# Two reorderings in a two-layer encoder kernel: the last chunk's activations before the last weight unit in every expert, and retention values projected feature-first, then turned

## The chip, the cores and the metric

The kernel runs on one core of one Trainium2 chip. The metric is the time of one execution in device microseconds, the median of several runs. Engines are called PE (TensorE's matmuls), PEld (TensorE's weight loads), DVE (VectorE), ACT (ScalarE), POOL (GpSimd) and SP (SyncE, which issues nearly all DMAs here).

## The reference

A trunk of two layers over 272 tokens (16 meta tokens and 256 frames) of width 1024. Each layer has a block with four retention heads and four latent-attention heads side by side, then a SwiGLU feed-forward; layer 0's is dense, layer 1's has 8 experts of which each token takes 2. Cut to what matters here:

```python
for layer in range(DEPTH):
    hn = rms_norm(h_res, attn_norm[layer])
    proj = hn @ w_in[layer]
    r_q, r_k, r_v, r_g, c_q, c_kv, k_rope = jnp.split(proj, IN_SPLITS, axis=-1)
    rv = to_heads(r_v, RET_HEADS)                     # the retention values
    y_ret = from_heads(head_rms(retention(rq, rk, rv)))
    y_mla = latent_attention(c_q, c_kv, k_rope, ...)  # softmax attention
    h_res = h_res + jnp.concatenate([y_ret * ..., y_mla * ...], axis=-1) @ w_out[layer]
    hn = rms_norm(h_res, ffn_norm[layer])
    # layer 0: dense; layer 1:
    for e in range(N_EXPERTS):
        out = out + gate_dense[..., e:e+1] * ((silu(hn @ w_gate[e]) * (hn @ w_up[e])) @ w_down[e])
```

## The kernel before, in words

**Numbers in two parts.** Every fp32 product is made of three fp32r matmuls (`mm3`): a high part times a high part, low times high, high times low. So each weight unit that comes from memory, 128 x 2048 numbers (1 MB), is first split: ACT copies it to `w_hi` (L919 in the attention and the dense part, L1110 in the experts), and DVE subtracts that copy from the unit and writes `w_lo` (L1178 and L1454). There are three split slots (`HSLOTS`). ACT may write a slot once PE has finished the unit that lay there (`w_used`), and PE may begin a unit once DVE has counted it in `split_lo`. SP refills a ring slot when the low part of its old unit is made. The engines run their own written order; nothing is scheduled by a tool.

**An expert** (8 of them, one after the other) takes its up to 128 tokens through 7 chunks of 512 hidden features. A chunk has four gate and up units (`g`, `u`) and two down units (`d`), of 12 matmuls of 512 columns each. PE's order is gate(c), transposes of the activations of chunk c-1 (`turn_hidden`), up(c), down(c-1); after chunk 6 only down(6) is left. The activations are made as gate x up by DVE (`a_moe`, L1466), turned by four PE transposes (`turn_hidden`, which signals `at_done`), copied to a high part by ACT (`hidden`, L1114) and given a low part by DVE (`hidden`, L1459, which signals `e_a`). down(c) waits for that. In the last chunk PE's order is: unit d(5,0); `turn_hidden(6)` and `turn_rows` (the next expert's tokens, 8 transposes); unit d(5,1); d(6,0); d(6,1). ACT and DVE go through one list of units, three ahead of PE: at the place of d(5,0) they split the last unit d(6,1) (`high_of`, `low_of`), then make the activations' parts (`hidden(6)`), then the next expert's tokens' parts (`take`, L1100 and L1438).

**The attention part of a layer.** Projections put features on partitions and 272 tokens in columns (`proj`: 24 matmuls of 272 columns, weights stationary), into a ring of four PSUM banks (`rot_bank`), from which ACT copies them out (`keep`, L957). The retention values are the exception: they are wanted with tokens on partitions, so `rv` is made in three token tiles (128, 128 and 16 tokens), each with the token tile stationary and 512 weight columns moving, 24 matmuls a tile. Between the tiles PE computes `latent_scores(2)` and `(3)`, on which DVE runs `mask_max` (L1240 to L1245) and ACT `exps` (L983); DVE's `normalise` (L1249, L1252) then makes them ready for `prob_transposes`, which follow the third tile on PE. After that come `proj("g0")`, the second transposes, and so on.

Of the kernel before, what the change touches and what calls it, by code (L numbers as in the profile page):

```python
# [41 lines left out]
P = 128  # L42
D = 1024
DK = D // P
# [5 lines left out]
HEADS = 4  # L50
# [10 lines left out]
UNIT = 2048  # L61
# [14 lines left out]
MOE_CHUNKS = DFF // 512  # L76
# [3 lines left out]
U_UQ, U_UKV, U_RV, U_RG, U_T1, U_T2, U_WO = 6, 7, 8, 10, 12, 13, 14  # L80
# [13 lines left out]
TILES = [(META, P), (META + P, P), (0, META)]  # L94
# [1 line left out]

OUTS = (["ckv", "kpe", "cq0", "cq1", "q0", "sckv", "scq", "q1", "q2", "q3", "k0", "k1", "k2", "k3",
# [3 lines left out]
N_OUTS = len(OUTS)  # L101

# [43 lines left out]
def build(nc, stream, h0, gains, router_w, fnorm, consts, out):  # L146
    with ExitStack() as ctx:
# [15 lines left out]
        hi = parts[:, 0:8 * L].rearrange("p (k t) -> p k t", k=8)  # L163
        lo = parts[:, 8 * L:16 * L].rearrange("p (k t) -> p k t", k=8)
# [28 lines left out]
        at = [0]  # L193
# [12 lines left out]
        rv, vm = carve3(3, 512), carve3(3, 512)  # L206
# [4 lines left out]
        std = carve3(HEADS, L)  # L211
# [37 lines left out]
        direct_used, split_hi, split_lo, w_used = sem("direct_used"), sem("split_hi"), sem("split_lo"), sem("w_used")  # L249
# [12 lines left out]
        out_done, out_free = sem("out_done"), sem("out_free")  # L262
# [49 lines left out]
        def split(eng, unit):  # L312

            n = SPLIT_OF[unit]
            eng.wait_ge(split_lo, n + 1)
            return w_hi[:, n % HSLOTS, :], w_lo[:, n % HSLOTS, :]
# [4 lines left out]
        def o_(name, layer):  # L321
            return layer * N_OUTS + OUTS.index(name)
# [150 lines left out]
        def _(pe):  # L473
            used_up = []
# [16 lines left out]
            def mm3(dst, sta, mov, start, stop, inc=None):  # L491

                mm(dst, sta[0], mov[0], start, False)
                mm(dst, sta[1], mov[0], False, False)
                mm(dst, sta[0], mov[1], False, stop, inc)
# [12 lines left out]
            def attention(layer):  # L508
                u0 = base_of(layer)
# [47 lines left out]
                def latent_scores(h):  # L557

                    dst = bank[6 + h % 2]
                    if h >= 2:  # L560
                        pe.wait_ge(sc_free, HEADS * layer + h - 1)
                    if h == 0:
                        pe.wait_ge(rope_done, N_ROPES * (layer + 1))
                        pe.wait_ge(out_free, o_("kn3", layer) + 1)
                    x = 64 * (h % 2)
                    for t, (c0, n) in enumerate([(0, META + P), (META + P, L), (MASK, META)]):
                        d = dst[0:TILES[t][1], c0:c0 + n]
                        mm(d, tok_rows(qn[:, h, :], t), kn[:, h, 0:n], True, False)
                        mm(d, tok_rows(qpe[x:x + 64, h // 2, :], t), kpe[x:x + 64, 0:n], False, True,
                           sc_done if t == 2 else None)  # L570
# [79 lines left out]
                w = slot(u0 + U_UKV)  # L650
                for h in range(HEADS):
                    mm(rot_bank(f"kn{h}"), w[:, h * P:(h + 1) * P], ckv, True, True, out_done)
                for t in range(3):
                    dst = rot_bank(f"v{t}", 512)[0:TILES[t][1], :]
                    mm(dst, tok_rows(ckv, t), w[:, 512:1024], True, True, out_done)
                used_up.append((direct_used, 1))
                latent_scores(0)
                latent_scores(1)
                for t in range(3):

                    p0 = TILES[t][0]
                    dst = rot_bank(f"rv{t}", 512)
                    for k in range(DK):
                        w = [x.rearrange("p (k c) -> p k c", k=4)[:, k % 4, :] for x in split(pe, u0 + U_RV + k // 4)]
                        mm3(dst, [hi[:, k, p0:p0 + P], lo[:, k, p0:p0 + P]], w, k == 0, k == DK - 1,
                            out_done if k == DK - 1 else None)
                    if t < 2:
                        latent_scores(2 + t)
                used_up.append((w_used, 2))
                prob_transposes(0)  # L670
                proj("g0", U_RG, 0)
                prob_transposes(1)
# [37 lines left out]
                p0 = 0 if layer == 0 else META  # L710
# [200 lines left out]
        def _(act):  # L911
# [36 lines left out]
            def attention(layer):  # L948
# [30 lines left out]
                def exps(h):  # L979
                    act.wait_ge(p1_ready, HEADS * layer + h + 1)  # L980
                    p = p_of(h)
                    for t, (rows, c0, c1) in enumerate([(P, 0, META + P), (P, META + P, MASK), (META, MASK, MASK + META)]):
                        x = A(p[0:rows, c0:c1], p[0:rows, c0:c1], ACT.Exp, bias=nmx[0:rows, h, t:t + 1], scale=SCALE,  # L983
                              accum_out=sums[0:rows, h, t:t + 1])
                    x.then_inc(exp_done, 1)
# [28 lines left out]
                    keep(f"v{t}", vm[0:rows, t, :], rows, 512)  # L1014
                exps(0)
                exps(1)
                for t, (_, rows) in enumerate(TILES):
                    keep(f"rv{t}", rv[0:rows, t, :], rows, 512)
                    if t < 2:
                        exps(2 + t)  # L1020
                high(b + 9)
                for name in OUTS[OUTS.index("g0"):]:
                    h = int(name[-1]) if name[-1].isdigit() else 0
# [78 lines left out]
            def expert(it):  # L1102
                def high_of(m):

                    n = MOE_SPLIT + m

                    act.wait_ge(slot_in[m % MOE_SLOTS], it * (16 * FFN_UNITS // MOE_SLOTS) + moe_arrivals(m))

                    act.wait_ge(w_used, it * FFN_UNITS + (n - HSLOTS + 1))
                    A(w_hi[:, n % HSLOTS, :], moe_slot(m), ACT.Copy).then_inc(split_hi, 1)  # L1110

                def hidden(c):
                    act.wait_ge(at_done, it * MOE_CHUNKS + c + 1)
                    A(ae_hi[c % 2], bank[6 if c < MOE_CHUNKS - 1 else 3][:, :], ACT.Copy).then_inc(e_ahi, 1)  # L1114

                scatter_copy(it)
                high_of(AHEAD)
                for m, (kind, c, i) in enumerate(MOE_ORDER[:-1]):
                    if (kind, i) == ("u", 1):
                        act.wait_ge(e_gu, it * MOE_CHUNKS + c + 1)  # L1120
                        A(sil_moe, bank[c % 2][:, :], ACT.Silu).then_inc(e_silu, 1)  # L1121
                    high_of(m + HSLOTS)
                    if (kind, i) == ("g", 1) and c:
                        hidden(c - 1)
                    if (kind, c, i) == ("d", MOE_CHUNKS - 2, 0):
                        hidden(c + 1)
                        take(it + 1)

            norm(0, mid=(0,), after=range(1, HSLOTS))
# [31 lines left out]
        def _(dve):  # L1161
# [43 lines left out]
            def attention(layer):  # L1205
                u0 = base_of(layer)
# [84 lines left out]
                    rope(r)  # L1291
                dve.wait_ge(ones_set, 4)
                arrived(dve, u0 + U_T1)
                for h in range(HEADS):
                    mask_max(h)
                for h in range(HEADS):
                    normalise(h)
                low(b + 9)
                low(b + 10)
# [8 lines left out]
                for h in range(HEADS):  # L1308
                    m = qn[:, h, :]
                    dve.wait_ge(out_free, o_(f"bM{h}", layer) + 1)  # L1310
                    x = V.scalar_tensor_tensor(out=m, in0=m, scalar=gain(G_MLA + 4 * layer + h), in1=std[:, h, :],
                                               op0=ALU.mult, op1=ALU.mult)
# [6 lines left out]
                for h in range(HEADS):  # L1319
                    m = qT[:, h, :]  # L1320
                    x = V.scalar_tensor_tensor(out=m, in0=m, scalar=gain(G_RET + 4 * layer + h), in1=rg[:, h, :],
                                               op0=ALU.mult, op1=ALU.mult)
# [8 lines left out]
                p0 = 0 if layer == 0 else META  # L1331
# [116 lines left out]
            def expert(it):  # L1448

                def low_of(m):  # L1450

                    n = MOE_SPLIT + m
                    dve.wait_ge(split_hi, it * FFN_UNITS + (n + 1))
                    V.tensor_tensor(w_lo[:, n % HSLOTS, :], moe_slot(m), w_hi[:, n % HSLOTS, :].bitcast(F32),  # L1454
                                    ALU.subtract).then_inc(split_lo, 1)

                def hidden(c):
                    dve.wait_ge(e_ahi, it * MOE_CHUNKS + c + 1)
                    V.tensor_tensor(ae_lo[c % 2], bank[6 if c < MOE_CHUNKS - 1 else 3][:, :], ae_hi[c % 2].bitcast(F32),  # L1459
                                    ALU.subtract).then_inc(e_a, 1)  # L1460

                low_of(AHEAD)
                for m, (kind, c, i) in enumerate(MOE_ORDER[:-1]):
                    if (kind, i) == ("u", 1):
                        dve.wait_ge(e_silu, it * MOE_CHUNKS + c + 1)
                        V.tensor_tensor(a_moe, bank[2 + c % 2][:, :], sil_moe, ALU.mult).then_inc(e_af, 1)  # L1466
                    low_of(m + HSLOTS)
                    if (kind, i) == ("g", 1) and c:
                        hidden(c - 1)
                    if (kind, c, i) == ("d", MOE_CHUNKS - 2, 0):  # L1470
                        hidden(c + 1)
                        take(it + 1)

            link(V.memset(rot, 0.0))
# [16 lines left out]
            for t in range(2):  # L1491
                x = V.tensor_scalar(G[:, t, :], col(C_IOTA, CAP), nxt[:, t:t + 1], None, ALU.is_equal)  # L1492
# [122 lines left out]
```

## Time and profile before

| | |
|---|---|
| median of 3 runs | 1569.68 us (1568.22 to 1570.18) |
| the profiled execution | 1569.67 us |
| its span, first to last instruction | 1567.9 us |
| PE busy | 1533.8 us, 98% of the span |
| DVE busy / ACT busy | 1207.4 us / 1010.3 us |
| mean granted TensorE clock | 0.996 of full |
| attention, layer 0 and layer 1 | about 15 to 162 us and 465 to 576 us |
| experts | 588 to 1551 us, one every 120.4 us |

How to read it: times in rows are microseconds from the start of the span. "Busy" of PE counts from the start of a matmul to its modelled end, and neighbours overlap: a matmul of 512 columns lasts 0.39 us in the records while the next one starts 0.23 us after it. So the distance from one start to the next is what a matmul costs in a row of them, and an idle time is read from starts.

### The profile page before, as it was taken

How to read it: one execution, taken by the hardware profiler on the slowest of the kernel's cores; microseconds unless marked ns; L12 is line 12 of the kernel's file. 1: busy time of each engine (PE TensorE's matmuls, PEld its weight loads, DVE VectorE, ACT ScalarE, POOL GpSimd, SP SyncE). 2: the span in 40 equal slices, each digit the busy share in tenths (PEclk: the TensorE clock that was granted, in tenths of full speed). 3: DMA queues.
4: the chain of work that ended last, by engine and by line, in shares of the span. 5: the costliest groups of instructions: out<-in, count | busy, mean ns of one | idle time of the engine just before them, and what ended most of it. 6: DMA issues, size and time to landing. Idle time of an engine off the chain costs nothing.

```text
span 1567.9 us, 21768 instructions
## 1 busy us (share of the span) xinstructions
PE 1533.8 (98%) x8368; PEld 1314.9 (84%) x8368; DVE 1207.4 (77%) x1015; ACT 1010.3 (64%) x938; POOL 35.3 (2%) x41
## 2 busy tenths in 40 slices
PE   9999999999999999999999999999999999999997
PEld 8778899999996798888887887887887887887885
DVE  5735566656684468888898888888888988888887
ACT  5645443333464557777777777777777777777775
POOL 0000000000000003000000000000000000000000
PEclk9999999999999999999999999999999999999998
DMA  8314444454333249999999999999999999999992
GB/s 335 133 69 162 149 175 161 164 191 184 128 122 134 90 155 363 397 350 391 370 355 388 372 361 385 381 355 377 372 376 365 384 376 354 394 376 348 420 359 109
DMA packets 64563, 447.91 MB, mean 286 GB/s; under 512 B 8105, under 2 KB 8137, under 8 KB 12160
## 3 DMA queue, kind: packets, MB, share of 16 engines
q1 hardware_dynamic: 61200, 438.02, 72.3%
q0 software_dynamic: 3312, 9.18, 2.1%
q8 instruction: 36, 0.59, 0.1%
q14 instruction: 15, 0.12, 0.0%
HBM read 442.20 MB, written 7.36 MB: 287 GB/s over the span
## 4 chain that ended last, share of the span: by engine, by line
PE 90%; DVE 4%; ACT 4%; issue 2%; DVEq 0%; ACTq 0%; POOL 0%; POOLq 0%
PE bank L485 88%; ACT w_hi L1110 2%; PE bank L489 2%; DVE w_lo L1454 1%; DVE sq L1195 0%; DVE scratch L1184 0%; DVE parts L1459 0%; ACT w_hi L919 0%; ACT scratch L1094 0%; DVE w_lo L1178 0%; DVE parts L1190 0%; ACT scratch L975 0%; ACT scratch L976 0%; DVE scratch L1403 0%; ACT scratch L957 0%
## 5 line engine op out<-in xcount | busy, mean ns | idle before, releaser
L485 PE MATMUL bank<-w_hi,parts 128*128 128x512 f32 x2784 | 866.3, 392 | 12.0 <-DVE parts L1459 8.8
L1454 DVE TENSOR_TENSOR w_lo<-ring,w_hi 128x2048 fp32r<-128x2048 f32 x288 | 659.7, 2293 | 105.2 <-ACT w_hi L1110 101.8
L1110 ACT ACTIVATE w_hi<-ring 128x2048 fp32r<-128x2048 f32 x288 | 551.9, 1919 | 187.3 <-PE bank L485 159.9
L485 PEld LDWEIGHTS bank<-w_hi,parts 128*128 128x128 f32 x2784 | 516.8, 188 | 123.2 <-DVE w_lo L1454 16.9
L485 PE MATMUL bank<-w_lo,parts 128*128 128x512 f32 x1392 | 542.9, 390 | 0.0
L485 PE MATMUL bank<-parts,w_hi 128*128 128x272 f32 (+1 forms) x2112 | 405.7, 290 | 6.1 <-DVE parts L1190 2.5
L485 PEld LDWEIGHTS bank<-parts,w_hi 128*128 128x128 f32 x2112 | 332.1, 188 | 9.0 <-DVE parts L1190 3.1
L485 PEld LDWEIGHTS bank<-w_lo,parts 128*128 128x128 f32 x1392 | 261.3, 188 | 55.5
L485 PE MATMUL bank<-parts,w_lo 128*128 128x272 f32 (+1 forms) x1056 | 303.3, 287 | 0.0
L1178 DVE TENSOR_TENSOR w_lo<-ring,w_hi 128x2048 fp32r<-128x2048 f32 x72 | 163.5, 2288 | 73.2 <-ACT w_hi L919 73.2
L485 PEld LDWEIGHTS bank<-parts,w_lo 128*128 128x128 f32 x1056 | 199.0, 188 | 0.4
L919 ACT ACTIVATE w_hi<-ring 128x2048 fp32r<-128x2048 f32 x72 | 137.5, 1912 | 89.8 <-PE bank L485 89.6
L1454 DVE TENSOR_TENSOR w_lo<-hT,w_hi 128x2048 fp32r<-128x2048 f32 x48 | 110.2, 2295 | 11.1 <-ACT w_hi L1110 9.2
L1110 ACT ACTIVATE w_hi<-hT 128x2048 fp32r<-128x2048 f32 x48 | 92.1, 1918 | 22.5 <-PE bank L485 13.6
L485 PE MATMUL bank<-scratch 128*128 128x128 f32 (+10 forms) x280 | 63.6, 355 | 1.3 <-issue 0.8
L485 PEld LDWEIGHTS bank<-scratch 128*128 128x128 f32 (+4 forms) x280 | 38.9, 175 | 28.4 <-issue 16.4
L1344 DVE TENSOR_TENSOR hT<-hT,bank 128x272 f32<-128x272 f32 x112 | 47.4, 435 | 16.8 <-PE bank L485 15.0
L1121 ACT ACTIVATE scratch<-bank 128x512 f32<-128x512 f32 x56 | 33.6, 599 | 32.1 <-PE bank L485 32.1
L489 PEld LDWEIGHTS bank<-c_sb,scratch 128*128 128x128 f32 x290 | 35.0, 141 | 10.5 <-issue 3.3
L489 PE MATMUL bank<-c_sb,scratch 128*128 128x128 f32 x290 | 40.9, 272 | 2.9 <-DVE scratch L1492 2.9
L1059 ACT ACTIVATE scratch<-bank 128x272 f32<-128x272 f32 x14 | 5.6, 398 | 54.0 <-PE bank L485 54.0
L1466 DVE TENSOR_TENSOR scratch<-bank,scratch 128x512 f32<-128x512 f32 x56 | 38.3, 685 | 0.0
(160 smaller groups left out, 626.6 us busy)
## 6 DMA issues: line engine op xcount, KB each, us to landing
ring<-stream SPq DMA_DIRECT2D x360, 1024.0 KB, 6.6
hT<-stream SPq DMA_DIRECT2D x48, 1024.0 KB, 7.0
ring<-stream SPq DMA_DIRECT2D x2, 976.0 KB, 4.7
ring<-stream SPq DMA_DIRECT2D x2, 768.0 KB, 9.9
c_sb<-consts SPq DMA_DIRECT2D x1, 1136.0 KB, 10.5
hT<-h SPq DMA_DIRECT2D x2, 544.0 KB, 4.4
ring<-stream SPq DMA_DIRECT2D x2, 544.0 KB
ring<-stream SPq DMA_DIRECT2D x2, 512.0 KB
```

What stands on the lines that cost most here:

```text
L485: return release(nc.tensor.matmul(dst, lhsT, rhs, start=start, stop=stop), inc)
L489: return release(nc.tensor.transpose(dst, src, ident[0:n, 0:n]), inc)
L919: A(w_hi[:, n % HSLOTS, :], slot(UNIT_OF[n]), ACT.Copy).then_inc(split_hi, 1)
L1059: A(sil_dense[:, 0, :], bank[0][:, 0:L], ACT.Silu)
L1110: A(w_hi[:, n % HSLOTS, :], moe_slot(m), ACT.Copy).then_inc(split_hi, 1)
L1121: A(sil_moe, bank[c % 2][:, :], ACT.Silu).then_inc(e_silu, 1)
L1178: V.tensor_tensor(w_lo[:, n % HSLOTS, :], slot(UNIT_OF[n]), w_hi[:, n % HSLOTS, :].bitcast(F32), ALU.subtract).then_inc(split_lo, 1)
L1344: V.tensor_tensor(hT[:, d, :], hT[:, d, :], bank[4 + d % 4][:, 0:L], ALU.add).then_inc(h_added, 1)
L1454: V.tensor_tensor(w_lo[:, n % HSLOTS, :], moe_slot(m), w_hi[:, n % HSLOTS, :].bitcast(F32), ALU.subtract).then_inc(split_lo, 1)
L1466: V.tensor_tensor(a_moe, bank[2 + c % 2][:, :], sil_moe, ALU.mult).then_inc(e_af, 1)
```

## The change

Three edits.

1. **Experts, last chunk.** At the place of unit d(5,0), ACT and DVE now first make the activations' parts (`hidden(6)`) and then split the last unit d(6,1); `take` stays third. PE's and SP's orders are the same.
2. **Retention values.** They are now projected like the others, head by head, weights stationary and 272 tokens moving (`rT0` to `rT3`, kept in `std`), and then turned by 12 PE transposes, four to each of the three token tiles. `latent_scores(2)` now comes after `rT1` and `latent_scores(3)` after `rT2`, and ACT's `exps(2)` and `exps(3)` behind the copies of `rT1` and `rT2`. The weights in memory are laid out to match. The two weight units are given back one by one (after `rT1` and `rT3`) instead of together.
3. **Softmax.** DVE's `normalise(0)` moves ahead of `mask_max(3)`.

```diff
+                for h in range(HEADS):
+                    proj(f"rT{h}", U_RV + h // 2, h % 2)
+                    if h in (1, 2):
+                        latent_scores(1 + h)
                 for t in range(3):
-                    p0 = TILES[t][0]
+                    p0, rows = TILES[t]
                     dst = rot_bank(f"rv{t}", 512)
-                    for k in range(DK):
-                        w = [... for x in split(pe, u0 + U_RV + k // 4)]
-                        mm3(dst, [hi[:, k, p0:p0 + P], lo[:, k, p0:p0 + P]], w, ...)
-                    if t < 2:
-                        latent_scores(2 + t)
-                used_up.append((w_used, 2))
+                    pe.wait_ge(out_free, o_("rT3", layer) + 1)
+                    for h in range(HEADS):
+                        turn(dst[0:rows, h * P:(h + 1) * P], std[:, h, p0:p0 + rows], ...)
...
+                for h in range(HEADS):
+                    keep(f"rT{h}", std[:, h, :])
+                    if h in (1, 2):
+                        exps(1 + h)
                 for t, (_, rows) in enumerate(TILES):
                     keep(f"rv{t}", rv[0:rows, t, :], rows, 512)
-                    if t < 2:
-                        exps(2 + t)
...  (ACT; the same edit with low_of on DVE)
+                    last = (kind, c, i) == ("d", MOE_CHUNKS - 2, 0)
+                    if last:
+                        hidden(c + 1)
                     high_of(m + HSLOTS)
                     if (kind, i) == ("g", 1) and c:
                         hidden(c - 1)
-                    if (kind, c, i) == ("d", MOE_CHUNKS - 2, 0):
-                        hidden(c + 1)
+                    if last:
                         take(it + 1)
...
-                for h in range(HEADS):
+                for h in range(HEADS - 1):
                     mask_max(h)
-                for h in range(HEADS):
+                normalise(0)
+                mask_max(HEADS - 1)
+                for h in range(1, HEADS):
                     normalise(h)
```

What stands in a row on ACT at the end of an expert before the change (bank3 holds the last chunk's turned activations, the `hT` ring slot the last unit, bank7 and bank6 the next expert's tokens):

```order
L1110 ACTIVATE w_hi<-ring 128x2048 [waits w_used]
L1107 REGISTER_ALU
L1109 REGISTER_ALU [waits slot_in6]
L1110 ACTIVATE w_hi<-hT 128x2048 [waits w_used]
L1114 ACTIVATE parts<-bank3 128x512 [waits at_done]
L1099 ISA
L1100 ACTIVATE parts<-bank7 128x512 [waits gt_done]
```

And after it:

```order
L1112 ACTIVATE w_hi<-ring 128x2048 [waits w_used]
L1116 ACTIVATE parts<-bank3 128x512 [waits at_done]
L1109 REGISTER_ALU
L1111 REGISTER_ALU [waits slot_in6]
L1112 ACTIVATE w_hi<-hT 128x2048 [waits w_used]
L1101 ISA
L1102 ACTIVATE parts<-bank7 128x512 [waits gt_done]
```

The copy of the activations has moved ahead of the last unit's copy; DVE's two subtractions have changed places in the same way, and each still stands behind ACT's copy of the same thing.

On PE, the end of the retention values before the change, the third token tile's last matmuls and the transposes behind it:

```order
L485 MATMUL bank<-w_hi,parts 128x512 x2
L485 MATMUL bank<-w_lo,parts 128x512
L489 MATMUL bank<-c_sb,sq 128x128 x3
L489 MATMUL bank<-c_sb,sq 16x16
L489 MATMUL bank<-c_sb,sq 16x128 x2
```

And after it, the last matmuls of `rT3`, the 12 new transposes (they read `std`, a part of `scratch`), and the old transposes of `sq`:

```order
L485 MATMUL bank<-parts,w_hi 128x272
L489 MATMUL bank<-c_sb,scratch 128x128 [waits out_free]
L489 MATMUL bank<-c_sb,scratch 128x128 x3
L489 MATMUL bank<-c_sb,scratch 128x128 [waits out_free]
L489 MATMUL bank<-c_sb,scratch 128x128 x3
L489 MATMUL bank<-c_sb,scratch 16x128 [waits out_free]
L489 MATMUL bank<-c_sb,scratch 16x128 x3
L489 MATMUL bank<-c_sb,sq 128x128 [waits p2_ready]
```

The new transposes stand between the last projection and the old ones, and the first of them waits for ACT's copy of `rT3`.

## Rows read from the trace of the kernel before

**Rows 1.** The page's busy times, with the share of the span and instructions.

```profile
PE 1533.8 (98%) x8368; PEld 1314.9 (84%) x8368; DVE 1207.4 (77%) x1015; ACT 1010.3 (64%) x938; POOL 35.3 (2%) x41
```

**Rows 2.** Waits of PE: engine, line <- waited for: us in total, times, longest.

```profile
PE bank L485 <- DVE parts L1459: 8.8, 8, 1.1
```

**Rows 3.** Timeline of PE, second expert's end: start, length, line, count.

```profile
818.64 1.47 PE L489 MATMUL bank<-c_sb,scratch 128*128 128x128 f32 x12
819.87 0.71 PE L485 MATMUL bank<-w_hi,parts 128*128 128x512 f32 x2
...
822.02 0.62 PE L485 MATMUL bank<-w_hi,parts 128*128 128x512 f32 x2
...
823.96 0.70 PE L485 MATMUL bank<-w_hi,parts 128*128 128x512 f32 x2 [1.10 <-DVE parts L1459]
...
824.73 0.62 PE L485 MATMUL bank<-w_hi,parts 128*128 128x512 f32 x2
...
829.50 0.62 PE L485 MATMUL bank<-w_hi,parts 128*128 128x512 f32 x2
```

**Rows 4.** Timeline of ACT, the same stretch.

```profile
818.95 1.93 ACT L1110 ACTIVATE w_hi<-hT 128x2048 fp32r<-128x2048 f32 x1 [0.43 <-PE bank L489]
820.77 0.58 ACT L1114 ACTIVATE parts<-bank 128x512 fp32r<-128x512 f32 x1
821.24 1.08 ACT L1100 ACTIVATE parts<-bank 128x512 fp32r<-128x512 f32 x2
824.47 1.92 ACT L1110 ACTIVATE w_hi<-ring 128x2048 fp32r<-128x2048 f32 x1 [2.14 <-PE bank L485]
```

**Rows 5.** Timeline of DVE, the same stretch.

```profile
818.55 2.29 DVE L1454 TENSOR_TENSOR w_lo<-ring,w_hi 128x2048 fp32r<-128x2048 f32 x1
820.90 2.31 DVE L1454 TENSOR_TENSOR w_lo<-hT,w_hi 128x2048 fp32r<-128x2048 f32 x1
823.13 0.68 DVE L1459 TENSOR_TENSOR parts<-bank,parts 128x512 fp32r<-128x512 f32 x1
823.74 1.27 DVE L1438 TENSOR_TENSOR parts<-bank,parts 128x512 fp32r<-128x512 f32 x2
826.42 2.29 DVE L1454 TENSOR_TENSOR w_lo<-ring,w_hi 128x2048 fp32r<-128x2048 f32 x1 [1.41 <-ACT w_hi L1110]
```

**Rows 6.** Timeline of PE in layer 0: retention values, transposes, projection g0.

```profile
73.25 0.73 PE L485 MATMUL bank<-w_hi,parts 128*128 128x512 f32 x2
...
89.32 0.73 PE L485 MATMUL bank<-w_hi,parts 128*128 128x512 f32 x2
...
94.99 0.92 PE L489 MATMUL bank<-c_sb,sq 128*128 128x128 f32 x6
95.66 0.37 PE L485 MATMUL bank<-parts,w_hi 128*128 128x272 f32 x1
...
98.76 0.92 PE L489 MATMUL bank<-c_sb,sq 128*128 128x128 f32 x6
```

**Rows 7.** Timeline of DVE and ACT in the same stretch: mask, exponentials, g0's copy.

```profile
89.42 0.59 DVE L1240 TENSOR_TENSOR sq<-bank,ring 128x416 f32<-128x416 f32 x1 [6.04 <-PE bank L485]
...
91.45 0.42 ACT L983 ACTIVATE sq<-sq,nmx 128x144 f32<-128x144 f32 x1 [3.71 <-DVE nmx L1245]
...
92.57 0.18 ACT L983 ACTIVATION_READ_ACCUMULATOR sq<-sq,nmx 16x1 f32 x1
...
98.96 0.40 ACT L957 ACTIVATE scratch<-bank 128x272 f32<-128x272 f32 x1 [1.39 <-PE bank L485]
```

**Rows 8.** Windows: stretch, length, busy of PE, PEld, DVE, ACT, POOL; PEclk, DMA share, GB/s.

```profile
579.00:582.00 3.00, 3.00 (x20) 3.00 (x20) 2.08 (x9) 2.55 (x4) 1.03 (x1) 0.67 0.08 11
714.98:835.32 120.34, 119.02 (x540) 98.07 (x540) 105.84 (x59) 89.44 (x60) 2.61 (x2) 1.00 0.98 371
840.00:850.00 10.00, 10.00 (x47) 8.27 (x46) 8.95 (x6) 7.29 (x6) 0.00 (x0) 1.00 1.01 417
```

More of the change, by code:

```diff
@@ L658, in attention @@
                 latent_scores(1)
+                for h in range(HEADS):
+                    proj(f"rT{h}", U_RV + h // 2, h % 2)
+                    if h in (1, 2):
+                        latent_scores(1 + h)
                 for t in range(3):
-                    p0 = TILES[t][0]
+                    p0, rows = TILES[t]
                     dst = rot_bank(f"rv{t}", 512)
-                    for k in range(DK):
-                        w = [x.rearrange("p (k c) -> p k c", k=4)[:, k % 4, :] for x in split(pe, u0 + U_RV + k // 4)]
-                        mm3(dst, [hi[:, k, p0:p0 + P], lo[:, k, p0:p0 + P]], w, k == 0, k == DK - 1,
-                            out_done if k == DK - 1 else None)
-                    if t < 2:
-                        latent_scores(2 + t)
-                used_up.append((w_used, 2))
+                    pe.wait_ge(out_free, o_("rT3", layer) + 1)
+                    for h in range(HEADS):
+                        turn(dst[0:rows, h * P:(h + 1) * P], std[:, h, p0:p0 + rows], out_done if h == HEADS - 1 else None)
                 prob_transposes(0)
@@ L1466, in expert @@
                         V.tensor_tensor(a_moe, bank[2 + c % 2][:, :], sil_moe, ALU.mult).then_inc(e_af, 1)
+                    last = (kind, c, i) == ("d", MOE_CHUNKS - 2, 0)
+                    if last:
+                        hidden(c + 1)
                     low_of(m + HSLOTS)
@@ L1469, in expert @@
                         hidden(c - 1)
-                    if (kind, c, i) == ("d", MOE_CHUNKS - 2, 0):
-                        hidden(c + 1)
+                    if last:
                         take(it + 1)
@@ L1570 @@
             units[at + 4 + i] = cols(rk[:, 256 * i:256 * (i + 1)])
-            units[at + U_RV + i] = rv[512 * i:512 * (i + 1)].reshape(4, P, 512).transpose(1, 0, 2).reshape(P, UNIT)
+            units[at + U_RV + i] = cols(rv[:, 256 * i:256 * (i + 1)])
             units[at + U_RG + i] = cols(rg[:, 256 * i:256 * (i + 1)])
```

2 rows, old and new, of the table OUTS are left out of this document.

## The prediction

> **What bounds the kernel now.** I began with the page's busy times: PE is busy for 98% of the span, DVE for 77%, ACT for 64% [rows 1]. Work that ACT or DVE saves is therefore worth nothing by itself. Time can be won in two ways only: fewer or shorter matmuls, or a pause of PE that goes away. The second view is the list of what PE waits for. One item stands above the rest: DVE's L1459, 8 waits of up to 1.1 us [rows 2], so one for each expert, at the same place. L1459 is the low part of the activations. The third view is the timeline of the three engines around one such wait [rows 3 to 5], and the fourth the stretch of layer 0 in which the retention values are made [rows 6, 7]. Last I looked at what the transfers and the clock do [rows 8].
>
> **Part 1: the experts' last chunk.** First the pause. The last triple of unit d(5,1) starts at 822.02 and the first of d(6,0) at 823.96. How fast triples follow in a row is seen between 824.73 and 829.50: 7 triples, 0.681 us each. Without a pause the second triple of d(6,0) would have started two triples behind 822.02, at 823.38; it started at 824.73 [rows 3]. The pause costs 1.35 us, somewhat more than the listed 1.1, because the matmul's modelled end hides a part and the first triple behind a pause is slower (0.77 us).
>
> What ends it? DVE finishes the last unit's low part at 823.21, then the activations' low part at 823.81 [rows 5], and PE starts 0.15 us later. The low part of d(6,0) itself was ready at 820.84 [rows 5]. So PE waits for the activations, and these stand on both engines behind the split of a unit that PE wants only a unit later.
>
> Now the new order, step by step. The 12 transposes take 818.64 to 819.87, 0.10 us each [rows 3]. ACT's split of the last unit starts at 818.95, on the first transpose's end [rows 4]; the fourth, which signals `at_done`, ends 0.31 us later, at 819.26. ACT copies the activations until 819.84 (0.58), then the last unit from 819.75 to 821.68 (1.93; neighbours on ACT overlap by 0.1), then the next tokens to 822.7 (1.08) [rows 4]. DVE is with d(6,0) until 820.84, makes the activations' low part until 821.5 (0.68), then the last unit's from 821.7 to 824.0 (2.31), then the tokens' until 825.2 (1.27) [rows 5]. PE reaches d(6,0) at 822.70 and finds everything ready for 1.2 us. It reaches d(6,1) 4 triples later, at 825.43, and the low part is there since 824.0. The pause is gone.
>
> What is late next? The next expert's first unit: ACT can start it 0.51 us behind the first matmul of d(6,0) (824.47 against 823.96 [rows 3, 4]), now at 823.21, so it is done at 825.1; DVE comes free at 825.2 and ends at 827.5; PE wants it at 829.50 - 1.35 = 828.15. A margin of 0.65 us, against 0.79 before (828.71 for 829.50 [rows 3, 5]). The units behind it hang on PE's own progress and keep their distance, and so does the wait that PE has at the third unit of the next expert. What queues behind the new wait for `at_done` on ACT is only the last unit's copy, on DVE only its subtraction, and these have 1.4 us to spare; SP refills that unit's slot 0.8 us later than now, with a whole round of seven slots before it is wanted. So 8 x 1.35 = **10.8 us**. From below the term is bounded by what the list of waits counts, 8.8 us; from above by nothing more than the pause.
>
> **Can the transfers follow?** An expert would take 119.0 us instead of 120.34, in which 371 GB/s are moved, with the DMA engines busy for 0.98 of it; at the same volume that asks for 375. In 840 to 850 the same queue moved 417 GB/s [rows 8]. I take the transfers for able to follow. The Trainium skill (DMA: Bandwidth & Descriptors, "Where 436 GB/s comes from") says that for transfers from HBM the memory side binds, near 358 GB/s for a core; by that rule the experts could not speed up at all. The trace disagrees by those two rows, but the rule is a rival below.
>
> **Part 2: the retention values.** A block of 24 matmuls of 512 columns takes from 89.32 to 94.99, 5.67 us, and there are three, the first from 73.25 [rows 6]; the third runs at full length although it has only 16 tokens. Removed: 17.0. Added: four blocks of 24 matmuls of 272 columns. Block g0 takes from 95.66 to 98.76, 3.10 us [rows 6]: 12.4. The two score computations between the blocks are as before. The 12 transposes have their like at the experts' end, 1.23 us [rows 3].
>
> Between `rT3` and the first transpose PE waits for ACT's copy. For g0 that copy starts 0.20 us behind the block's end and lasts 0.40 [rows 6, 7]. But `exps(3)` stand ahead of it: the scores end at 89.32, the mask begins at 89.42, the exponentials run from 91.45 to 92.75 [rows 7], 3.43 us behind the scores. The block takes 3.10, so the copy starts 0.33 behind the block instead of 0.20, ends at 0.73, and PE goes on at about **0.75**. `normalise(0)`, now ahead of that mask on DVE, falls into the 6.04 us for which DVE idles there [rows 7]; it costs nothing, and it brings nothing, since the transposes that want it come 3 us later. Where that cover fails it costs the 0.8 us it lasts.
>
> Behind the transposes, ACT copies three tiles out and splits a unit, some 3.7 us, and `g0`'s copy is wanted over 5 us behind the first transpose; the four new copies of `rT` fall where ACT has nothing to do. Each layer: 17.0 - 12.4 - 1.23 - 0.75 = 2.6 us. PE is what ends this stretch and nearly all after it, so I count it in full, twice: **5.2 us**. Bounds: 0 if what follows holds the same end, 6.7 with no pause at all.
>
> **The sum.** 10.8 + 5.2 = 16.0 from the profiled execution's 1569.67 gives 1553.7; the median of the runs, 1569.68, is the same.
>
> **The rivals.**
> A. *The attention's gain is lost*: once PE comes earlier, something that does not move with it is late, such as a transfer of tables or of the output weights. For it: there is nothing I can show. Against: the units that follow were loaded long before. 1569.67 - 10.8 = 1558.9.
> B. *The next expert's first unit takes the pause's place.* Its margin is the smallest I found, 0.65 us, and rests on DVE's chain of last unit, tokens, first unit. If it is late by 0.5 us the experts give 8 x 0.85 = 6.8 and the sum is 1557.7.
> C. *The transfers bind* and an expert stays at 120.34 us: only 5.2 are won, 1564.5. For it: 0.98 busy. Against: 417 GB/s.
> D. *The clock falls* at the pause before the transposes. In 579 to 582, behind a wait and a few tiny matmuls, the granted clock was 0.67, a mixture of 2.4 and 1.2 GHz [rows 8]. Two thirds of 3 us at the lower level and the like of it behind cost under 2 us each time, twice a kernel: 1557.5. Against: the new pause is shorter and stands among dense blocks. The Trainium skill (TensorE: Matmul & The Clock Gate, "What's actually happening") calls the lower clock the state of rest that activity lifts; the row agrees.
> E. *Slower*: the last unit, now second, and what is chained to it on DVE come later than I have them. Place: the end of each expert. Price: 8 us for each us beyond the margin of 0.65. It eats the whole gain at 2.0 us beyond, and passes +0.2% at 2.4; with 2.5 the time is 1573.7. Against: the row durations would have to be wrong by 3 us in a chain of 6.
>
> That the change doesn't do what it says would need PE to wait for the unit d(6,0) and not for the activations; its low part was 3.1 us old when PE started, so I leave that at next to nothing, inside C.
>
> **How the numbers follow.** Chances: the forecast 0.72 (1551.5 to 1556), A 0.08, B 0.08, C 0.04, D 0.04, E 0.04. The forecast's case with A, B and D makes 0.92; the range of 1551.5 to 1560 holds them, and I take 0.8 of it for sure since in each case the size may be off. A measurement of this kernel tells some 0.2%, 3.1 us, from no change. All cases but E lie beyond that on the fast side, C by 5 us; I leave 0.02 for no difference, 0.04 for slower, 0.94 for faster.
>
> **What would show it.** Part 1: PE's waits for the activations' low part are gone from its list, PE's triples run on from d(5,1) to d(6,0), and an expert takes 119.0 us. If B holds, PE waits 8 times at an expert's first unit. If C holds, ACT waits for DMAs. Part 2: from the first matmul of `rT0` to the transposes of the probabilities 19.1 us instead of 21.7; a wait of 0.75 us for the copy before the new transposes; the same in layer 1. The prediction is wrong if 512-column blocks are gone and the layer is no shorter.

## The result and the profile after

The changed kernel takes 1554.09 us (median of 4 executions, 1553.72 to 1556.38), the kernel before, on the same chip and in turn with it, 1569.93 (4 executions, 1568.22 to 1571.46). The ratio is 0.9902, with an interval of 0.9885 to 0.9920: 15.4 us less, between 12.6 and 18.1. The prediction's 16.0 lies in that. The profiled execution of after is the one of 1553.72 us; its span is 1551.9.

The page's busy times, answering to [rows 1]:

```profile
PE 1525.3 (98%) x8440; PEld 1314.6 (85%) x8440; DVE 1206.1 (78%) x1015; ACT 1012.5 (65%) x946; POOL 35.0 (2%) x41
```

PE has 72 matmuls more and is busy for 8.5 us less, and its share of the span is still 98%. So of the 16.0 us between the two profiled executions about half is shorter work and the other half is time in which PE stood still. The page alone does not say more.

The list of what PE waits for (in all, times, longest) answers to [rows 2]:

```profile
PE bank L489 <- DVE scratch L1500: 2.9, 1, 2.9
...
PE bank L485 <- DVE w_lo L1460: 1.5, 7, 0.2
PE bank L489 <- ACT scratch L957: 1.2, 2, 0.6
```

The item that led it, the activations' low part (L1465 now), is not in it at all. New is the last line: two waits of 0.6 us, one in each layer, for the copy ahead of the new transposes. The 7 waits of 0.2 us, at an expert's third unit, were there before.

**The experts.** PE's timeline at the second expert's end, answering to [rows 3] (start, length, line, count, idle before):

```profile
811.19 1.47 PE L489 MATMUL bank<-c_sb,scratch 128*128 128x128 f32 x12
812.42 0.70 PE L485 MATMUL bank<-w_hi,parts 128*128 128x512 f32 x2
...
815.25 0.61 PE L485 MATMUL bank<-w_hi,parts 128*128 128x512 f32 x2
...
820.69 0.61 PE L485 MATMUL bank<-w_hi,parts 128*128 128x512 f32 x2
...
825.45 0.61 PE L485 MATMUL bank<-w_hi,parts 128*128 128x512 f32 x2
...
826.50 0.73 PE L485 MATMUL bank<-w_hi,parts 128*128 128x512 f32 x2 [0.22 <-DVE w_lo L1460]
```

From the first triple of d(5,1), at 812.42, to 825.45 the triples follow each other every 0.68 us (the first takes 0.77), and no row between them has a wait; d(6,0) begins at 815.25. The next pause is the 0.22 us at 826.50, the third unit of the next expert. ACT and DVE in the same stretch, answering to [rows 4, 5]:

```profile
811.83 0.60 ACT L1116 ACTIVATE parts<-bank 128x512 fp32r<-128x512 f32 x1 [0.76 <-PE bank L489]
812.32 1.91 ACT L1112 ACTIVATE w_hi<-hT 128x2048 fp32r<-128x2048 f32 x1
...
815.67 1.92 ACT L1112 ACTIVATE w_hi<-ring 128x2048 fp32r<-128x2048 f32 x1 [0.47 <-PE bank L485]
```

```profile
813.31 0.69 DVE L1465 TENSOR_TENSOR parts<-bank,parts 128x512 fp32r<-128x512 f32 x1
814.26 2.29 DVE L1460 TENSOR_TENSOR w_lo<-hT,w_hi 128x2048 fp32r<-128x2048 f32 x1 [0.26 <-ACT w_hi L1112]
...
817.67 2.28 DVE L1460 TENSOR_TENSOR w_lo<-ring,w_hi 128x2048 fp32r<-128x2048 f32 x1
```

The activations' low part ends at 814.00, and PE wants it at 815.25. The next expert's first unit ends at 819.95 and PE wants it at 820.69: a margin of 0.7 us. What an expert takes is the distance between equal pieces of the chain of work. Of before, then of after (start, length, what):

```profile
714.98 11.20 PE bank L485 x48
...
1437.15 11.20 PE bank L485 x48
```

```profile
707.54 11.20 PE bank L485 x48
...
1421.40 11.20 PE bank L485 x48
```

Over the six experts between the first and the last of these, before took 120.36 each and after 118.98: 1.38 us less. Over the eight that is 11.1 us.

**The retention values.** PE's timeline of layer 0, answering to [rows 6], and ACT's, to [rows 7]:

```profile
89.26 0.29 PE L485 MATMUL bank<-parts,w_hi 128*128 128x272 f32 x1
90.13 1.50 PE L489 MATMUL bank<-c_sb,scratch 128*128 128x128 f32 x12 [0.58 <-ACT scratch L957]
91.47 0.92 PE L489 MATMUL bank<-c_sb,sq 128*128 128x128 f32 x6
```

```profile
89.51 0.19 ACT L983 ACTIVATION_READ_ACCUMULATOR sq<-sq,nmx 16x1 f32 x1
89.60 0.38 ACT L957 ACTIVATE scratch<-bank 128x272 f32<-128x272 f32 x1
```

The last matmul of `rT3` starts at 89.26, 0.13 us before the next could, and the transposes start at 90.13: a pause of 0.74. It ends with ACT's copy of `rT3`. In ACT's order that copy stands behind the six instructions of `exps(3)`, but it came hardly later for them: it starts 0.21 us behind the block's end (89.39), and g0's copy of before, ahead of which ACT was idle, started 0.20 us behind its block's end [rows 6, 7]. The pause is thus 0.21 us to the copy's start, 0.38 for the copy, and 0.15 from its end to the first transpose. From the first matmul of `rT0`, at 72.23, to the transposes of the probabilities, at 91.47, it is 19.24 us, where the prediction had 19.1 and before took 21.74. The whole stretch, in the chain of work of before and of after:

```profile
64.50 30.65 PE bank L485 x130
...
95.91 3.02 PE bank L485 x24
```

```profile
63.49 22.85 PE bank L485 x130
...
90.13 2.26 PE bank L489 x18
92.38 3.02 PE bank L485 x24
```

From the same first matmul to the end of g0's block: 34.43 us before, 31.91 after, so 2.52 less. In layer 1 the same pieces give 34.44 (478.96 to 513.40) and 31.92 (475.45 to 507.37).

**The account.** 11.1 + 2 x 2.52 = 16.1 of the 15.95 us between the two profiled executions. The rest are two stretches that the change does not touch, and that nearly cancel. At the start, the first piece of the chain is shorter, by 0.96 us; at the end, the last matmuls are longer, by 0.83, and so are the two transposes ahead of them, by 0.25 (0.66 instead of 0.41). 16.1 + 0.96 - 0.83 - 0.25 = 16.0, the difference of the spans. The first two rows are of before, the others of after:

```profile
1.13 8.80 PE bank L485 x36
...
1555.68 5.41 PE bank L485 x8
```

```profile
1.13 7.84 PE bank L485 x36
...
1538.84 6.24 PE bank L485 x8
```

The end is the clock: in the 8 us around those last matmuls the mean granted clock was 0.79 of full before and 0.57 after, mixtures of 2.4 and 1.2 GHz in both. For the start the clock's rows show nothing, 1.00 in both; it stays unexplained. A kernel with the attention of before (`e3_vector_swap_only`, below) also had the shorter start.

**The transfers.** One expert of after, answering to the second of [rows 8] (stretch, length, busy of PE, PEld, DVE, ACT, POOL; clock, DMA share, GB/s):

```profile
707.54:826.50 118.96, 118.75 (x540) 98.13 (x540) 105.69 (x59) 89.45 (x60) 2.62 (x2) 1.00 0.96 377
```

377 GB/s where 371 were moved before, and no wait for a DMA appeared. The Trainium skill (DMA: Bandwidth & Descriptors, "Where 436 GB/s comes from") has the memory side bind near 358 GB/s for a core; the measurement, on a chip of which one core runs, disagrees.

### The profile page after: what moved, and what is told of

The parts are those of the page before. It is cut to its first block, busy times and chain, and to the rows that moved or that the text cites. A ratio compares the mean times of both kernels' runs of the same rounds, so it can differ in the third digit from the quotient of the medians.

```text
span 1551.9 us, 21926 instructions
## 1 busy us (share of the span) xinstructions
PE 1525.3 (98%) x8440; PEld 1314.6 (85%) x8440; DVE 1206.1 (78%) x1015; ACT 1012.5 (65%) x946; POOL 35.0 (2%) x41
## 4 chain that ended last, share of the span: by engine, by line
PE 92%; DVE 4%; ACT 3%; issue 1%; ACTq 0%; DVEq 0%; POOL 0%; POOLq 0%
PE bank L485 89%; PE bank L489 3%; DVE w_lo L1460 1%; ACT w_hi L1112 1%; DVE sq L1199 0%; DVE scratch L1188 0%; ACT scratch L1096 0%; ACT w_hi L919 0%; DVE w_lo L1182 0%; DVE parts L1194 0%; ACT scratch L975 0%; ACT scratch L976 0%; DVE scratch L1409 0%; ACT scratch L957 0%; ACT sq L983 0%
## 5 line engine op out<-in xcount | busy, mean ns | idle before, releaser
L485 PE MATMUL bank<-w_hi,parts 128*128 128x512 f32 x2688 | 834.5, 392 | 3.3 <-DVE parts L1444 1.6
L485 PEld LDWEIGHTS bank<-w_hi,parts 128*128 128x128 f32 x2688 | 499.7, 188 | 108.0 <-DVE w_lo L1460 5.0
L485 PE MATMUL bank<-w_lo,parts 128*128 128x512 f32 x1344 | 523.8, 390 | 0.0
L485 PE MATMUL bank<-parts,w_hi 128*128 128x272 f32 (+1 forms) x2240 | 431.5, 291 | 6.1 <-DVE parts L1194 2.4
L485 PEld LDWEIGHTS bank<-parts,w_hi 128*128 128x128 f32 x2240 | 352.4, 188 | 9.2 <-DVE parts L1194 3.0
L485 PE MATMUL bank<-parts,w_lo 128*128 128x272 f32 (+1 forms) x1120 | 321.7, 287 | 0.0
L485 PEld LDWEIGHTS bank<-w_lo,parts 128*128 128x128 f32 x1344 | 252.2, 188 | 53.2
L485 PEld LDWEIGHTS bank<-parts,w_lo 128*128 128x128 f32 x1120 | 211.0, 188 | 0.4
L1112 ACT ACTIVATE w_hi<-hT 128x2048 fp32r<-128x2048 f32 x48 | 91.9, 1915 | 19.1 <-PE bank L485 13.7
L489 PE MATMUL bank<-c_sb,scratch 128*128 128x128 f32 (+1 forms) x314 | 44.1, 273 | 4.1 <-DVE scratch L1500 2.9
L489 PEld LDWEIGHTS bank<-c_sb,scratch 128*128 128x128 f32 (+1 forms) x314 | 37.4, 140 | 12.2 <-issue 3.3
```

The lines of the kernel that those rows point to most:

```text
L485: return release(nc.tensor.matmul(dst, lhsT, rhs, start=start, stop=stop), inc)
L489: return release(nc.tensor.transpose(dst, src, ident[0:n, 0:n]), inc)
```

## The experiments

All are timed in turn with the kernel before. Savings are (1 - ratio) x 1569.9. The first four take the change apart.

### The two parts alone

`e1_experts_only` is the kernel before with edit 1 alone (the new order on ACT and DVE); of this kernel only times are used. `e2_retention_only` is the kernel after with edit 1 undone on both engines:

```diff
-                    last = (kind, c, i) == ("d", MOE_CHUNKS - 2, 0)
-                    if last:
-                        hidden(c + 1)
                     high_of(m + HSLOTS)          # low_of on DVE
                     ...
-                    if last:
+                    if (kind, c, i) == ("d", MOE_CHUNKS - 2, 0):
+                        hidden(c + 1)
                         take(it + 1)
```

> The kernel before with the experts' edit alone (activations before the last unit, on ScalarE and VectorE). Theory, the two terms are separate and add: an expert takes 118.98 us instead of 120.37, 8 x 1.38 = 11.1 us less, so about 1558.8 against 1569.9. Rival, part of the experts' gain needed the attention's shift (another phase of the transfers): fewer than 8 us. Rival, the retention edit does all beyond 8.8 us: 1561.

> The kernel before with the retention values' and the softmax edit alone. Theory: 2.5 us less in each layer, 5.0 in all, 1564.9, and 8 waits of 1.1 us for the activations' low part still there. Rival, the layers' gain was luck of the clock at the start (the profile after began 1.0 us earlier before any edited line): then 1566 to 1570.

Measured: `e1_experts_only` 0.9931 [0.9919, 0.9943], 10.8 us less; `e2_retention_only` 0.9969 [0.9959, 0.9979], 4.9 us less. Predicted were 10.8 and 5.2. The two add up to 15.7, against 15.4 for both together, so neither part needs or spoils the other. In `e2_retention_only` PE's list of waits shows the old item, untouched:

```profile
PE bank L485 <- DVE parts L1463: 8.7, 8, 1.1
```

### One engine's order alone

Which engine's order made the pause? `e3_vector_swap_only` has the new order on DVE only, `e4_scalar_swap_only` on ACT only, both on the kernel before. The edit is the one of edit 1, in DVE's or in ACT's function.

> The kernel before with the experts' edit on VectorE alone; ScalarE still copies the last unit first. Theory, what holds TensorE is VectorE's 2.3 us subtraction of the last unit ahead of the activations': ScalarE's copy of the activations ends at 821.35 in the times of before, VectorE's subtraction at 822.05, TensorE wants it at 822.70. So the pause is gone with this half alone: as e1, 1558.8. Rival, both copies have to be swapped (the activations' copy on ScalarE is what comes late): a pause stays, 1563 to 1570.

> The kernel before with the experts' edit on ScalarE alone; VectorE still subtracts the last unit first, and now starts it 0.8 us later. Theory: the activations' low part ends at 824.7 instead of 823.8, the pause grows from 1.35 to 2.2 us: 8 x 0.87 = 7 us slower than before, 1576.9. Rival, the order on ScalarE is what counts: faster than before, down to 1559.

`e3_vector_swap_only`: 0.9936 [0.9923, 0.9949], 10.0 us less, not to be told from both orders together by the time. By its trace an expert takes 118.98 us (714.11 to 1428.00 for six), as in after. Its DVE timeline:

```profile
820.52 0.69 DVE L1459 TENSOR_TENSOR parts<-bank,parts 128x512 fp32r<-128x512 f32 x1 [0.53 <-ACT parts L1114]
```

ACT still makes the activations' copy 1.5 us later than in after (2.13 us behind the transposes' first start instead of 0.64), and DVE waits 0.53 us for it. But the low part ends at 821.21, and PE wants it at 821.84, where d(6,0) begins: 0.6 us to spare. So DVE's order alone is the cause of the pause and its cure; ACT's turns a spare 0.6 us into 1.2.

`e4_scalar_swap_only` went the other way: 1.0109 [1.0094, 1.0124], 17 us slower, where 7 had been expected. Its PE list of waits, PE's timeline at the second expert's end, and 12 us around that end (columns as above):

```profile
PE bank L485 <- DVE parts L1461: 15.1, 8, 1.9
```

```profile
826.12 0.70 PE L485 MATMUL bank<-w_hi,parts 128*128 128x512 f32 x2 [1.89 <-DVE parts L1461]
...
827.77 1.05 PE L485 MATMUL bank<-w_hi,parts 128*128 128x512 f32 x2
...
829.05 1.05 PE L485 MATMUL bank<-w_hi,parts 128*128 128x512 f32 x2
```

```profile
821.00:833.00 12.00, 10.12 (x40) 7.92 (x39) 7.68 (x7) 6.85 (x6) 1.03 (x1) 0.86 0.94 376
```

The expected part is there: the pause is listed with 1.9 us instead of 1.1, 8 times, and the experts without anything else take 121.14 us, 0.78 more than before (0.87 expected). The rest is the clock. From the third triple behind the pause they start 1.28 us apart (827.77, 829.05) instead of 0.68, which is the 1.2 GHz level, and the stretch had a mean granted clock of 0.86. It happened behind 3 of the 8 pauses; those experts took 122.77, so it cost 1.6 us each time. 8 x 0.78 + 3 x 1.6 = 11.0, and this profiled execution took 1581.4, 11.7 more than before's. The other executions took 1586 to 1589 at mean clocks of 0.988 to 0.991, against 0.992 here: more such falls, by the clock; they have no trace that shows where.

### The retention part's terms

`e5_normalise_back` undoes edit 3 alone, in after:

```diff
-                for h in range(HEADS - 1):
+                for h in range(HEADS):
                     mask_max(h)
-                normalise(0)
-                mask_max(HEADS - 1)
-                for h in range(1, HEADS):
+                for h in range(HEADS):
                     normalise(h)
```

> The changed kernel with the softmax order put back (all masks, then all normalisations). Theory, the move is free and idle: 1554.1, and the transposes of the probabilities wait for nothing, since the first normalisation would be done 1.2 us before they come. Rival, it carries part of the gain: up to 1.6 us more.

Measured: 0.9904 [0.9889, 0.9919], 1555.29 us. No change, as expected, and in its trace the stretch of layer 0 takes 31.91 us, as in after: edit 3 is worth nothing either way.

`e6_turns_twice` does the new transposes of every token tile twice (the second time the same results to the same place), which prices them by themselves:

```diff
-                    for h in range(HEADS):
-                        turn(dst[0:rows, ...], std[:, h, p0:p0 + rows], out_done if h == HEADS - 1 else None)
+                    for rep in range(2):
+                        for h in range(HEADS):
+                            turn(dst[0:rows, ...], std[:, h, p0:p0 + rows],
+                                 out_done if rep and h == HEADS - 1 else None)
```

> The changed kernel with the 12 new transposes of each layer done twice. Theory, they stand on the path at 1.34 us a dozen less what a pipeline start costs: 2 x 1.23 = 2.5 us more, 1556.6. Rival, they are partly hidden behind a later wait (for ScalarE's tables): 0 to 1 us more.

Measured: 0.9919 [0.9905, 0.9933], 1558.67 us, 2.7 less saved than after. The chain of work in layer 0:

```profile
90.91 3.57 PE bank L489 x30
```

30 transposes in 3.57 us against 18 in 2.26: 12 more cost 1.31 a layer, 0.109 each, in both layers 2.6. They lie in full on the path, as the sum had them, and are 0.1 us dearer than the 1.23 that was taken from the experts' end.

`e8_probs_before_turns` asks whether the pause before the transposes can be had for nothing, by putting the next matmuls of PE into it:

```diff
+                prob_transposes(0)
                 for t in range(3):
                     ...
-                prob_transposes(0)
```

> The changed kernel with the first transposes of the probabilities between the last projection and the new transposes. Theory: they fill 0.67 us of the 0.74 us for which TensorE waits for the copy: 2 x 0.65 = 1.3 us less, 1552.8. Rival, the new transposes then come 0.6 us later to ScalarE, and something behind is late: no gain.

In the trace the pause is gone. The chain of layer 0 runs through it: the 130 matmuls of after and the 24 of `rT3` are one piece.

```profile
64.27 26.06 PE bank L485 x154
...
92.41 3.03 PE bank L485 x24
```

From the same first matmul to the end of g0's block: 31.17 us, 0.74 less than after. Timed: 0.9894 [0.9881, 0.9908], by the ratios 1.3 us more saved than after, as 2 x 0.74 would have it; but the intervals overlap, and its median, 1554.84 us, is not below after's 1554.09, so the time proves no gain. The profiled execution shows where the 1.5 us went. In the matmuls ahead of the experts the granted clock was low (0.72 in 564 to 570), where after's was at full. The same 24 matmuls, of after and of this kernel:

```profile
566.73 2.84 PE bank L485 x24
```

```profile
566.00 4.35 PE bank L485 x24
```

### What is late next in an expert

The prediction gave the next expert's first unit a margin of 0.65 us and priced everything beyond at 8 us for each us (rivals B and E). Three kernels that are otherwise the kernel after put 1, 3 and 4 unused subtractions of 128 x 512 on DVE behind the tokens' parts, in `take` (0.6 us each):

```diff
+                for i in range(1):               # 3 and 4 in the others
+                    V.tensor_tensor(sq[:, 512 * i:512 * (i + 1)], bank[6][:, :], <x_hi, 512 columns>, ALU.subtract)
```

> The changed kernel with one more subtraction of 0.64 us on VectorE behind the next tokens' low part, ahead of the next expert's first unit (its result is used by nothing). That unit's low part ended 0.73 us before TensorE wanted it in the profile after. Theory, the margin is real: the experts take 118.98 us as before, and only the first, once, starts 0.6 us later: 1554.7. Rival, the experts' end is tighter than it looks: up to 5 us more.

> The same with three more, 1.83 us. Theory: the first unit comes 1.1 us late in each expert, 8 x 1.2 = 9.6 us more and 1.8 once: 1565.5. The pause is as long as the one of the kernel before, which left the clock alone, so the clock stays. Rival, the clock falls here too: 13 us more, 1578.

> The same with four more, 2.44 us: TensorE pauses 1.7 us at each expert's first unit. If the fall of the clock seen with ScalarE's half alone (a pause of 1.9 us, then triples of 1.28 us instead of 0.68) comes with the length of the pause: 8 x 1.8 + 2.4 + 8 x 1.6 = 30 us more, 1584. If that place or its transposes made it fall, not the length: 17 us more, 1571.

With one: 0.9899 [0.9882, 0.9915], 1554.4 us, and an expert takes 118.97 us. No change, so a margin of at least 0.6 is real. With three: 0.9952 [0.9936, 0.9969], 1563.2 us; with four: 0.9992 [0.9983, 1.0002], 1568.7 us. Both cost less than expected (1565.5, and 1571 at the least). PE's waits and the timeline, first with three, then with four:

```profile
PE bank L485 <- DVE w_lo L1463: 6.6, 7, 1.0
PE bank L485 <- DVE sq L1447: 4.2, 1, 4.2
PE bank L489 <- DVE scratch L1503: 4.2, 1, 4.2
```

```profile
825.05 0.62 PE L485 MATMUL bank<-w_hi,parts 128*128 128x512 f32 x2
...
826.84 0.73 PE L485 MATMUL bank<-w_hi,parts 128*128 128x512 f32 x2 [0.95 <-DVE w_lo L1463]
```

```profile
825.33 0.62 PE L485 MATMUL bank<-w_hi,parts 128*128 128x512 f32 x2
...
827.71 0.73 PE L485 MATMUL bank<-w_hi,parts 128*128 128x512 f32 x2 [1.54 <-DVE w_lo L1463]
```

The place is the one that rival B named, an expert's first unit. With three the unit starts 1.79 us behind the last triple instead of 0.68, so 1.11 late; with four 2.38, so 1.70 late. But an expert grew only by 0.72 (to 119.70) and by 1.32 (to 120.30, from 827.71 to 948.02). The difference is nearly the same in both, 0.39 and 0.38, and it is the wait that after has at the third unit: there the next triple starts 1.05 us behind 825.45 instead of 0.68, 0.37 late. That unit hangs on the end of the expert before, and where the first unit is late it comes in time: with three, one piece of the chain runs on for 72 matmuls through the place where after's chain begins anew.

```profile
826.84 16.62 PE bank L485 x72
```

So the first 0.37 us of lateness replace a wait that PE has anyway. The account with three, against after: the wait ahead of the first expert +2.6 (4.2 instead of 1.6), a lower clock behind it +2.0, seven experts 7 x 0.72 = +5.0; at the end a wait of 4.2 instead of 2.9, +1.3, the wait at the last expert's third unit -0.4, and shorter last matmuls (5.28 instead of 6.24, and the two before them) -1.2. Together 9.3, with 9.4 between the spans.

Nor did the clock fall inside the experts, with a listed pause of 1.5 us at seven places.

### Two better versions

`e7_unit_before_scatter` takes the wait at the third unit away. On ACT the unit is split ahead of the weighting of the last expert's output rows:

```diff
-                scatter_copy(it)
                 high_of(AHEAD)
+                scatter_copy(it)
```

> The changed kernel, and at each expert's start ScalarE copies the third unit before it scales the last expert's rows out. It aims at the wait left in each expert, between the third triple from the end of the second unit (825.45) and the next (826.50), 0.37 us, and the slow triple behind it, 0.13. Theory: the unit is ready 1.4 us earlier, the wait is gone, 8 x 0.5 = 4.0 us less, 1550.1. Rival, the rows' scaling, now late, delays what follows on ScalarE (the fourth unit): no gain or a loss of some us.

Measured: 1551.09 us, 0.9873 [0.9858, 0.9889], 19.9 saved, 4.6 more than after by the ratios and 3.0 less time by the medians. The chain runs through a whole expert without leaving PE; here is the piece over the place of the third unit's wait:

```profile
1051.62 24.54 PE bank L485 x108
```

An expert takes 118.46 us (1042.12 to 1160.58), 0.52 less than in after. There are seven such places, from the second expert on, so the trace carries 3.6 us; at the first expert's third unit a wait of 0.2 stays. `e11_both` has this edit and the one of `e8_probs_before_turns`:

> The changed kernel with both additions, the third unit before the rows' scaling and the first transposes of the probabilities before the new ones. Theory, they add: 4.3 us (an expert takes 118.46 instead of 118.98) and 1.5 us (0.75 in each layer), 0.9865 of before, 1548.5.

Measured: 1550.02 us (1549.36 to 1550.47), 0.9869 [0.9853, 0.9886], 20.6 saved. It has the lowest median, 4.1 us below after's, and none of its executions overlaps with after's; that it beats `e7_unit_before_scatter` is not shown, the intervals overlap nearly in full. Its expert takes 118.44 and its stretch in layer 0 is as in `e8_probs_before_turns`; a part was lost between, where its granted clock in the 25 us ahead of the experts was 0.86, like that of `e7_unit_before_scatter`, and after's 0.93.

## Why the prediction was right

- **What bounds the kernel.** PE, and only pauses or matmuls count. `e3_vector_swap_only` shows it best: ACT's order can be left as it was, DVE then waits 0.53 us, and nothing is lost.
- **The pause and what ends it.** Read as 1.35 from starts (8.8 / 8 = 1.1 by the list), measured as 1.38. The step that named the activations' parts behind the last unit is shown, and narrowed: it was DVE's order. The low part stood behind a subtraction of 2.3 us; ACT's copy, 1.5 us late, was still soon enough. The prediction moved both and did not tell them apart.
- **The new order.** The activations' copy starts 0.64 us behind the transposes' first start (0.62 in the working) and the low part ends 1.25 us before PE wants it (1.2). The margin of the next first unit is 0.7 (0.65).
- **The transfers** follow at 377 GB/s; rival C is out.
- **The retention values.** 17.0 - 12.4 stands. The pause was 0.74 (0.75), but that figure is luck: two of its terms were off and cancelled. The copy started 0.21 us behind the block instead of 0.33, because the working let it start at the end of `exps(3)` and left out the overlap of 0.1 us between neighbours on ACT that it had used for the experts; and PE started 0.15 us behind the copy's end, which the working took as 0.02. So `exps(3)` added 0.01 us at most to the pause. The transposes were mis-sized: 1.23 taken from the experts' end, 1.34 here by starts (90.13 to 91.47), 1.31 in `e6_turns_twice`. So 2.52 a layer instead of 2.6, 5.0 in all; `e2_retention_only` gives 4.9. All of it reached the end, so rival A is out.
- **`normalise(0)`** costs and brings nothing, as said (`e5_normalise_back`).
- **Rival D**, a fall of the clock at the new pause, did not come: the pause of 0.74 left it at full.
- **Rivals B and E had the right place and a wrong price.** "8 us for each us beyond the margin" leaves out that PE waits for the third unit anyway; the first 0.37 us beyond the margin are nearly free. The working had that wait in view and said it would keep its distance; that holds only as long as the first unit is in time.
- **By luck.** Beside the pause above: the total hit 16.0 within 0.05 in the profiled executions. The experts came out 0.3 higher, the layers 0.2 lower, and two differences of 1 us, at the start and at the end, cancelled. By the ratio's interval the size is known to 3 us only; the traces' distances carry the terms.

## What to carry to other kernels

Where two engines work through the same list and a third waits, find out which of their orders holds the wait: here reordering the subtracting engine alone gave all of it, and reordering the copying engine alone made the kernel slower. When a pause is priced, read it from starts, and look for the waits further on that the same lateness would fill: they are a discount on every delay, and once the delay is gone they are the next thing to take (0.5 us an expert here). An unused instruction of known length on the suspected engine measures a margin that a trace can only suggest.

## What the runs showed of the hardware

A pause of PE can cost more than its length, when the clock falls behind it. Two places bear on it. At an expert's end, 8 listed pauses of 1.9 us were followed by a fall in 3 cases, for 1.6 us each; 7 of 1.5 us and 8 of 1.1 us in none. Ahead of the first expert, after's pause of 1.6 us was followed by none, and with one subtraction more, 2.2 us, the clock fell, and cost about 1.6 us again; behind 4.2 and 3.9 us, with three and four more, it was low too. But at the same place a longer pause, 2.44 us in `e2_retention_only` and 2.43 in `e8_probs_before_turns`, left the clock at full. So the length of the pause alone does not decide. The stretch of 8 us, of after, of `e9_vector_plus1` and of `e2_retention_only`, columns as above, and the last one's pause:

```profile
582.00:590.00 8.00, 7.15 (x30) 5.63 (x31) 6.09 (x15) 5.88 (x5) 3.92 (x3) 1.00 0.71 252
```

```profile
582.00:590.00 8.00, 6.75 (x23) 5.42 (x24) 5.16 (x15) 4.94 (x4) 3.37 (x3) 0.79 0.71 253
```

```profile
582.00:590.00 8.00, 6.54 (x28) 5.10 (x28) 6.07 (x16) 5.57 (x6) 3.62 (x2) 1.00 0.72 273
```

```profile
583.32 0.72 PE L485 MATMUL bank<-w_hi,parts 128*128 128x512 f32 x2 [2.44 <-DVE parts L1442]
```

Each is one execution, and what else decides stays open.

What a low clock costs depends on what it meets. In `e8_probs_before_turns` it met matmuls on the chain of work and cost 1.5 us (4.35 instead of 2.84, above). In after the granted clock was low in 574 to 578 (0.57), but the matmuls there end well before PE's next wait, for DVE: their 0.8 us more only shortened that wait, from 2.4 us in `e8_probs_before_turns` to 1.6.

The executions of one kernel also differ among themselves with their mean clock: those of `e1_experts_only` took 1556.9 to 1557.0 us at 0.998 and 1560.4 to 1561.8 at 0.994 to 0.995. None of these six has a trace, so what made that difference is not known; a low clock at another place is one candidate. The difference is what limits all the times above to some 2 us.
